# Sixteen meta keys of eight heads turned together, value sums kept per group, and four reordered places in a two-block kernel

## What is computed

```python
def causal_block_attention(q, k, v, scale, cum=None):      # L = 16 meta + 256 real
    def attend(qb, qpos, cq=None):
        s = jnp.einsum('bhqd,bhkd->bhqk', qb, k) * scale
        if cq is not None:
            s = s + (cq[..., :, None] - cum[:, :, None, :])
        s = jnp.where(key_pos[None, :] <= qpos[:, None], s, -jnp.inf)
        p = jax.nn.softmax(s, axis=-1)
        return jnp.einsum('bhqk,bhkd->bhqd', p, v)
...
o_mla = causal_block_attention(q_m, k_m, v_mla, MLA_SCALE)
y_mla = (o_mla * jax.nn.silu(z_mla)) @ w_br_mla[l]
o_fox = causal_block_attention(fq, fk, fv, FOX_SCALE, cum)
y_fox = (o_fox * jax.nn.silu(z_fox)) @ w_br_fox[l]
mixed = (jax.nn.sigmoid(gate_a) * y_mla + jax.nn.sigmoid(gate_b) * y_fox) @ w_out[l]
h = h + rmsnorm_2(mixed, post_norm_g[l])
```

```python
hs = hs * lax.rsqrt(jnp.mean(hs * hs, axis=-1, keepdims=True) + EPS)   # per head
return (hs * norm_w * o_gate) @ w_out
```

## Time and profile before

| | us |
|---|---|
| median of 3 runs | 1001.35 |
| their range | 1000.96 to 1002.16 |
| the profiled execution | 1001.34 |
| its span, first to last instruction | 999.5 |
| PE busy | 957.9 |
| DVE busy | 592.5 |
| ACT busy | 482.3 |
| POOL busy | 22.6 |

### The profile page before, as it was taken

How to read it: one execution, slowest core, us unless ns; L and a number is a source line. 1 busy time by engine, 2 the same in 40 slices (tenths; PEclk the granted TensorE clock), 3 DMA queues, 4 the chain that set the end, 5 groups by cost and what they waited for, 6 DMA issues and landing times.

```text
span 999.5 us, 14170 instructions
## 1 busy us (share of the span) xinstructions
PE 957.9 (96%) x5243; PEld 802.3 (80%) x5243; DVE 592.5 (59%) x1103; ACT 482.3 (48%) x768; POOL 22.6 (2%) x41
## 2 busy tenths in 40 slices
PE   6999799999999999999999999999999999999996
PEld 6877587888888899778888888879988887887875
DVE  4856657745455578556453635776554655665565
ACT  5545546535353447454443434675344444434542
POOL 0003100000000000000000000000000000000000
PEclk9999999999999999999999999999999999999998
DMA  6642245463645522246545464322233233333441
GB/s 215 237 169 85 84 184 180 161 230 148 224 153 198 181 85 86 85 150 224 212 150 228 145 233 173 123 106 107 92 120 127 85 127 127 133 120 127 153 163 43
DMA packets 25319, 149.25 MB, mean 149 GB/s; under 512 B 2992, under 2 KB 3120, under 8 KB 11056
## 3 DMA queue, kind: packets, MB, share of 16 engines
q1 hardware_dynamic: 24624, 146.39, 40.2%
q0 software_dynamic: 640, 2.11, 0.7%
HBM read 147.45 MB, written 1.05 MB: 149 GB/s over the span
## 4 chain that ended last, share of the span: by engine, by line
PE 73%; DVE 7%; ACT 5%; DVEq 3%; issue 2%; ACTq 0%
PE bank L435 21%; PE bank L436 21%; PE bank L437 21%; ACT w_hi L1184 2%; PE bank L506 1%; DVEq L2058 1%; DVE w_lo L1705 1%; PE bank L700 1%; DVE arena L2083 1%; PE bank L983 1%; PE bank L968 1%; PE bank L815 1%; PE bank L1004 1%; PE bank L1005 1%; PE bank L1003 1%
## 5 line engine op out<-in xcount | busy, mean ns | idle before, releaser
L435 PE MATMUL bank<-w_hi,x_hi 128*128 128x512 f32 (+2 forms) x648 | 262.7, 405 | 3.7 <-DVE ffn_nat L1955 1.4
L436 PE MATMUL bank<-w_lo,x_hi 128*128 128x512 f32 (+2 forms) x648 | 254.1, 392 | 0.0
L437 PE MATMUL bank<-w_hi,x_lo 128*128 128x512 f32 (+2 forms) x648 | 252.0, 389 | 0.0
L1619 DVE TENSOR_TENSOR w_lo<-w_raw,w_hi 128x2048 fp32r<-128x2048 f32 x52 | 118.8, 2292 | 62.2 <-ACT w_hi L1123 61.2
L435 PEld LDWEIGHTS bank<-w_hi,x_hi 128*128 128x128 f32 x648 | 122.3, 189 | 33.2 <-issue 5.8
L1705 DVE TENSOR_TENSOR w_lo<-w_raw,w_hi 128x2048 fp32r<-128x2048 f32 x50 | 114.4, 2290 | 51.3 <-ACT w_hi L1184 50.6
L437 PEld LDWEIGHTS bank<-w_hi,x_lo 128*128 128x128 f32 x648 | 121.7, 188 | 27.1
L436 PEld LDWEIGHTS bank<-w_lo,x_hi 128*128 128x128 f32 x648 | 122.0, 188 | 22.4
L1123 ACT ACTIVATE w_hi<-w_raw 128x2048 fp32r<-128x2048 f32 x54 | 103.1, 1916 | 58.4 <-DMA w_raw<-w_main_dram 51.5
L1184 ACT ACTIVATE w_hi<-w_raw 128x2048 fp32r<-128x2048 f32 x50 | 95.0, 1908 | 13.9 <-PE bank L437 9.6
L1323 ACT ACTIVATE ffn_nat<-bank,stat 128x256 f32<-128x256 f32 x44 | 20.8, 473 | 134.2 <-PE bank L437 134.1
(11 more groups left out here) (349 smaller groups left out, 1526.1 us busy)
## 6 DMA issues: line engine op xcount, KB each, us to landing
w_raw<-w_main_dram SPq DMA_DIRECT2D x111, 1024.0 KB, 4.9
s_raw<-w_side_dram SPq DMA_DIRECT2D x51, 512.0 KB, 4.2
h<-x_dram SPq DMA_DIRECT2D x2, 512.0 KB, 3.9
w_raw<-w_main_dram SPq DMA_DIRECT2D x2, 512.0 KB, 6.7
arena<-rows_dram POOLq DMA_DIRECT2D x2, 512.0 KB, 4.1
out_dram<-arena SPq DMA_DIRECT2D x1, 512.0 KB, 2.6
out_dram<-arena SPq DMA_DIRECT2D x2, 256.0 KB, 2.0
arena<-c_b_dram POOLq DMA_DIRECT2D x1, 264.0 KB, 2.8
```

The lines of the kernel that those rows point to most:

```text
L435: pe.matmul(out, ah, bh, start=first, stop=False)
L436: pe.matmul(out, ah, bl, start=False, stop=False)
L437: return pe.matmul(out, al, bh, start=False, stop=last)
L1619: dve.tensor_tensor(w_lo[:, slot, 4 * g:4 * g + 4, :], w_raw[:, g, :, :], w_hi[:, slot, 4 * g:4 * g + 4, :], ALU.subtract).then_inc(w_lo_o ...
```

## The change

It has five parts.

1. First keys: DVE takes the rest of the first half of chunk 1 ahead of the root, and PE turns the root after the first half of the first key matmuls.
2. Recurrent heads: two gate tiles stand ahead of the scores, and the two state matmuls go one behind the other into banks 5 and 7.
3. Output product: the loop is written out. The matmuls of tiles 2 and 3 stand ahead of the turns of tiles 4 and 5; ACT makes tiles 2 and 3 ahead of weights; the gating of heads 2 and 3 signals after each head.
4. Last loop, first heads: the first key block is the first thing in step 0; the side unit of the queries goes ahead of a weight half on DVE; both halves of chunk 39 are split in step 2.
5. Last loop, all heads: `turn` has three transposes and `values` three matmuls. ACT copies the 16 meta columns of each head into a tile of eight heads by 16 keys (`meta_kept`). After eight heads this tile is turned at once (`meta_turn`, two transposes), copied (`meta_turned`) and multiplied by meta values of eight heads set out on a block diagonal (`meta_values`, two matmuls of 512 columns). The diagonal is made by `spread`, a matmul that repeats 16 rows eight times and a DVE product with a mask, once for each 512 columns, in steps 1, 2, 7 and 10. The sums of eight heads stay in banks 6 and 7, and DVE scales them at once (`group_out`).

The core of the diff:

```diff
+GROUP = 8
+SPREADS = {1: ("um", 0), 2: ("um", 1), 7: ("fm", 0), 10: ("fm", 1)}
+def after_rider(n):
+    extra = [SPREADS[n]] if n in SPREADS else []
+    if n and n % GROUP == 0 or n == 2 * NH - 1:
+        extra.append(("mt", n // GROUP if n == 2 * NH - 1 else n // GROUP - 1))
+    return extra
-        keys += RIDERS[n]
+        keys += RIDERS[n][0:1] + after_rider(n) + RIDERS[n][1:]
-        HALVES.setdefault(_at + 1, []).append((_c, 1))
+        HALVES.setdefault(_at + (_c != C_FK + 3), []).append((_c, 1))
+        c_bank = (bank[5], bank[7])
-            pool.memset(f_vm, 0.0).then_inc(vz_ok, 1)
-            pool.memset(v_mm, 0.0).then_inc(vz_ok, 1)
...
+            for k0 in (0, KT // 2):
+                for i in range(2):
+                    for k in range(k0, k0 + KT // 2):
+                        ins = halves_tile(C_MK, None, 2 * i, k, to=bank[6 + i])
+                    if k0:
+                        ins.then_inc(mk_ps, 1)
+                    elif i == 0:
+                        pe.wait_ge(r0_ok, 1)
...
+                gate_part(0, 2)
                 if hh:
                     pe.wait_ge(hf_ok, 2 * hh)
...
-                    pe.matmul(bank[5][:, 0:VW], m_kw[:, d, :], v_aug[:, d, hh, :], ...)
-                    gate_part(beside[d], beside[d + 1])
+                    pe.matmul(c_bank[d][:, 0:VW], m_kw[:, d, :], v_aug[:, d, hh, :], ...)
...
-            streamed("m_out", xn, {4: lambda: pe.wait_ge(xn_ready, 2)}, [m_out_tiles], ahead=False)
+            for k in range(KT):
+                st_wait("m_out", k)
+                if k in (0, 1):
+                    to_stationary("m_out", xn, None, 0, ks=(k + 2,))
+                elif k in (4, 5):
+                    to_stationary("m_out", xn, xn_ready, 3, ks=(k + 2,))
+                m_out_tiles(k)
+                if k == 3:
+                    to_stationary("m_out", xn, xn_ready, 2, ks=(4, 5))
...
-                pe.transpose(bank[5][:, 2 * P:3 * P], s_[:, 2 * M + 2 * P:416], ident[:, :])
-                pe.transpose(bank[6][:, 0:P], s_[:, 0:P], ident[:, :])
-                pe.transpose(bank[6][:, P:2 * P], s_[:, M + P:M + 2 * P], ident[:, :]).then_inc(pt_ps, 1)
+                pe.transpose(bank[5][:, 2 * P:3 * P], s_[:, 2 * M + 2 * P:416], ident[:, :]).then_inc(pt_ps, 1)
+            def values(n, v):
+                pe.wait_ge(pt_ok, A2 + n + 1)
+                first = n % GROUP == 0
+                if first and n:
+                    pe.wait_ge(og_ok, n // GROUP)
+                at = slice(n % GROUP * HD, (n % GROUP + 1) * HD)
+                pe.matmul(bank[6][:, at], pt[:, 0:P], v(0), start=first, stop=False)
+                pe.matmul(bank[7][:, at], pt[:, P:2 * P], v(0), start=first, stop=False)
+                pe.matmul(bank[7][:, at], pt[:, 2 * P:3 * P], v(1), start=False, stop=False)
+            def meta_turn(g):
+                b = acc_wait(("mt", g))
+                pe.wait_ge(mp_ok, GROUP * (g + 1))
+                for r in range(R):
+                    ins = pe.transpose(b[:, r * P:(r + 1) * P], meta_p[g][:, r, :], ident[:, :])
+                done(ins, ("mt", g))
+            def meta_values(g):
+                evacuated(("mt", g), (("um", "fm")[g // 2], g % 2))
+                for r in range(R):
+                    ins = pe.matmul(bank[6 + r][:, :], pt[:, 384 + r * P:384 + (r + 1) * P], meta_v[g], start=False, stop=True)
+                ins.then_inc(og_ps, 1)
+            def spread(key):
+                b = acc_wait(key)
...
+                done(pe.matmul(b[:, :], repeat[0:M, :], src[0:M, key[1] * CH:(key[1] + 1) * CH], start=True, stop=True), key)
...
+                if n == 0:
+                    riders(RIDERS[n], 0)
...
+                last = n % GROUP == 0 and n // GROUP
+                if last:
+                    meta_turn(last - 1)
                 if n:
                     head_values(n - 1)
                 turn(A2 + n)
+                if n in SPREADS:
+                    spread(SPREADS[n])
+                if last:
+                    meta_values(last - 1)
+                if n == 2 * NH - 1:
+                    meta_turn(n // GROUP)
...
             head_values(2 * NH - 1)
+            meta_values(2 * NH // GROUP - 1)
...
+            def meta_kept(n):
+                act.drain()
+                kept = sm[:, n % 2, 0:2 * (M + P)].rearrange("p (r x) -> p r x", r=R)[:, :, 0:M]
+                at = slice(n % GROUP * M, (n % GROUP + 1) * M)
+                act.activation(meta_p[n // GROUP][:, :, at], kept, ACT.Copy).then_inc(mp_ok, 1)
-                meta_turned(A2 + n)
+                meta_kept(n)
+                if n and n % GROUP == 0 or n == 2 * NH - 1:
+                    meta_turned(after_rider(n)[-1][1])
...
             rest_side(0)
+            rest_half(1, 1, 0)
             rstd("x0", [(R, D)])
...
-                ins.then_inc(xn_ready, 1)
+                    if hh:
+                        ins.then_inc(xn_ready, 1)
...
+            rest_side(U_Q)
             rest_half(C_FK + 1, (C_FK + 1) % 2, 1)
-            rest_side(U_Q)
...
+                if n >= 2:
+                    dve.wait_ge(mp_ok, n - 1)
+            def group_out(g):
+                dve.wait_ge(og_ps, g + 1)
+                dve.drain()
...
-                    head_out(n - 1)
+                    head_root(n - 1)
                 dve.wait_ge(pt_ps, A2 + n + 1)
                 dve.tensor_copy(pt[:, 0:384], bank[5][:, 0:384]).then_inc(pt_ok, 1)
+                if n in SPREADS:
+                    spread(SPREADS[n])
+                if n and n % GROUP == 0:
+                    group_out(n // GROUP - 1)
```

More of the change, by code:

```diff
@@ L1268, in _ @@
                     act.wait_ge(c_ps, 2 * hh + d + 1)
-                    act.activation(m_c[:, d, :], bank[5][:, 0:VW], ACT.Copy).then_inc(c_ok, 1)
+                    act.activation(m_c[:, d, :], c_bank[d][:, 0:VW], ACT.Copy).then_inc(c_ok, 1)
                 if hh < H0 - 1:
@@ L1280, in _ @@
             squares(H0 - 1)
[L1281 removed]
+            split_st("m_out", m2_tile, lambda k: pcol("mlstm_norm", k), ks=(2, 3))
+            split_both("m_out", lambda k: pcol("mlstm_norm", k), C_MO + 3, 1, first=4, hi=m2_tile)
             def mixer_out(name, c, ffn_st, gain):
@@ L1807, in gated @@
                 dve.wait_ge(og1_ok, 2 * pair + 2)
-                for r in range(R):
-                    for hh in (2 * pair, 2 * pair + 1):
+                for hh in (2 * pair, 2 * pair + 1):
+                    for r in range(R):
                         xs = XN[:, r, hh * DV:(hh + 1) * DV]
```

111 lines of the change are left out of this document (64 added, 47 removed).

## The result

The changed kernel takes 1014.83 us (median of 4 runs, 1013.98 to 1016.51) against 1001.55 us (4 runs, 1000.96 to 1002.16) of the kernel before: ratio 1.0135, 95% interval 1.0117 to 1.0152. I had forecast 1003.7 and the range ended at 1008.5. The direction was right. The time lies outside the range.

The account below looks back on a forecast made before the run. PE, busy 96% of the span, plus its stands was taken as the bound. Terms summed to +0.2 us on 1001.35, plus 2.2 for one clock fall: 1003.7 us, own range 1000.5 to 1006.5, 8 in 10 from 994.5 to 1008.5.

Parts of the forecast that it names:

- Work of the loop: PE work over 32 heads: 0.67 us less a head, twelve 512-column matmuls and eight transposes added; net -10.2 us.
- Stands of the loop: Last loop: new PE waits at spreads, group ends and riders, plus lost savings, less one removed wait; +16.6 us.
- group end n=8: Last loop: meta value sums wait for ACT's turned meta keys, which stand behind the exps of head 9; 2.25 us.
- second rider of n=3: Last loop: the moved half of chunk 39 puts 2.3 us of DVE ahead of mask and query; +1.25 us.
- Recurrent heads: Recurrent mixer: gate tiles cover the stand at the scores, a second state bank removes another; -1.6 us.
- Output product: Mixer's output: tiles 2 and 3 issued ahead of the 4.77 us wait, gating signalled earlier; -4.9 us.
- First heads: Start of the last loop: query rest ahead of a weight rest, first key block ahead of scores; -0.5 us.
- First keys: Second value chunk: DVE is late, so PE's stand there grows to some 3 us; +0.8 us.
- term of the clock: Stands of 3.85, 2.95 and 3 us in loop and second value chunk: one clock fall, at +2.2 us.
- second rival: Clock falls at all three long stands: 6.6 us instead of 2.2, 1008 us; chance 0.15.
- first rival: Loop: ACT and DVE come sooner, waits at group ends and spreads halve, clock holds; 995.5 us, chance 0.25.
- rival of dear 512-column matmuls: Loop: 512 f32 columns cost twice the price, or value matmuls were covered by weight loads; 1014 us, chance 0.04.

Follow-up runs that it names:

- reorderings alone: Kernel before with the first keys, recurrent heads, output product and first heads changed, without the grouped meta keys: 997.1 us, ratio 0.9952.
- filled stands: Changed kernel with f32 matmuls of a zero weight added on PE inside four loop stands (n=7, 10, 16, 24): 1007.2 us.
- joined kernel with the new first keys: The joined kernel, but with the changed kernel's order of the first keys: 996.6 us.
- gate steps: The joined kernel with the last two gate-tile steps of the last two recurrent heads moved ahead of the fourth value matmul: 993.3 us.
- joined: Changed kernel with ACT's copy ahead of exps, Fox spreads behind riders n=14 and 15, n=8 meta turn and sums later, old first keys: 991.7 us, ratio 0.9896.
- fastest kernel: The joined kernel with spreads behind the riders of n=7, 10, 11 and 14 and over 128 rows: 988.2 us, ratio 0.9866.

## Why the prediction was wrong

Each term of the sum, by the lags of the table:

- Work of the loop: 0.67 us less a head was forecast; the lag falls by 0.66 to 0.69 at the heads from n=11 to n=15 and by 0.60 to 0.69 after n=17, but where a tile rest stands. A pair of sums costs what I had from the earlier trace rows: 0.86 each, 1.88 us for two with the last one's end. A spread costs some 0.3 us more than that: the one of n=2 begins at 693.84 in the changed kernel and the second product behind it at 695.12, 1.28 us later, where 0.86 and a step of 0.12 would be 0.98.
- Stands of the loop. They came about as long as the rows said, together 0.7 us shorter, and one of them elsewhere:

| place | forecast | measured |
|---|---|---|
| spread n=1 | 0.65 | 0.74 |
| spread n=7 | 1.65 | 1.54 |
| group end n=8 | 2.25 | 1.57 |
| spread n=10 | 1.65 | 1.91 |
| group end n=16 | 3.85 | 3.70 |
| group end n=24 | 2.95 | 2.83 |
| three tile rests, each more than before | 0.6 | 0.70, 0.73, 0.71 |
| second rider of n=3 | 1.25 | 0.95 |

The one at n=8 is not the wait that I had described: I expected the value sums to wait for ACT's copy, and PE stood at the turn of the meta keys ahead of them, for the accumulator that DVE frees. The sums did not wait.

- Recurrent heads: -1.6 forecast. The lag falls by 2.2 up to 96.87. But DVE does its root and its weight rest there no sooner, and a stand of 1.59 us at 102.2 took the place of 0.53. In the kernel with the reorderings alone, which has no fall in the way, the heads give -2.9.
- Output product: -4.9 forecast, -4.4 in that kernel, with the stand of 0.96 us that I had at 0.9, and full clock. The -5.8 of the table hold the 1.5 us that come back from the fall at 104.
- First heads: -0.5 forecast, -0.3 measured.
- First keys: +0.8 forecast, with a stand of some 3 us. The stand is 3.18 us; the lag at 56.26 is +1.58, less the 0.36 of the start +1.2. The clock comes on top, 1.6 us.

The loop without its slow stretches: 18.6 less the 9.1 of the filled stands are 9.5, where I had 6.4. The weight rest at 713.68 gave 1.65 where I had 1.5. The 3.1 us that are missing do not lie in the stands. From turn to turn of the probabilities, the five steps with a late spread or a group end (n=7, 8, 10, 16, 24) take 0.5 to 1.0 us more than their stands, their new matmuls and their fall, 3.2 together. Some 0.6 of that are the two spreads in them, by the price above; for the rest my sum has no term, and no run separates what it is. All terms together without the clock miss by +0.4 - 1.3 + 0.5 + 0.2 + 3.1 = +2.9 us.

The step that failed is the term of the clock: "Three lengths lie between; I take one fall, at +2.2." I had two points, a stand of 4.77 us that had a fall behind it and one of 1.50 that had none, and counted as endangered only the three stands near 3 us and above. Measured were six falls, behind 3.18, 1.59, 1.54, 1.91, 3.70 and 2.83 us, that took 1.6, 0.1, 1.6, 3.2, 1.4 and 3.0 us, with the unrounded figures 10.8 in all, 9.1 of it in the loop. With 8.6 too little for the clock, 2.9 for the other terms and 0.4 for the start, 1003.7 becomes 1015.6; the profiled run took 1015.5 and the median is 1014.8. Two errors lie in the 8.6. The three long stands all fell, with 5.9 us instead of 2.2: that is the second rival, which I gave 0.15 and 1008. And 4.9 us came behind three stands of 1.5 to 1.9 us, two of which I had priced by their length and not asked about the clock, although they lay above the one length that I knew to be harmless; the third, at 102, I had not seen, and it cost 0.1. The filled stands show that the 9.1 us of the loop are the clock, not the stands.

The first rival (waits half of mine) fell with the table above. Its argument, that ACT and DVE are half idle, was true and beside the point: ACT stood idle 3.19 us ahead of the exps with the copy behind them in its queue. I had written down that the copy stands behind the exps and took it as given; the remedy was in that sentence. The rival of dear 512-column matmuls named 1014, close to the measured time, by luck: they cost 0.86 us each, not twice that.

## What to carry to other kernels

When a change puts new waits on an engine that was busy 96% of the time, list every stand of about 1.5 us and more that it makes and price each one twice: its own length, and what the clock may take behind it, here 1.4 to 3.2 us where PE had work until the next wait was past, and 0.1 where a wait for ACT of 1.57 us followed and took it up. Before judging an idea by such a version, look at what the releasing engine does ahead of the release: here fewer small matmuls lost 21 us on their own, much of it because a ready copy of 0.36 us stood behind exps in ACT's order (moving it gave 11.7) and because the spreads stood where an accumulator came late. With both moved, and with the same first keys, the grouped keys cost nothing; the spreads behind riders and over 128 rows gave another 3.5 us. Measure a clock effect by filling the stand with work of no use, and read the cost from matched matmuls past the next wait, not from the length of the slow stretch.

## What the runs showed of the hardware

- After the first 12 us, all 16 stands of 2.37 us and more in the traces of this study have a stretch at 1.2 GHz that begins in them or right behind; of those between 1.54 and 1.97 us some were and some not, in code that is the same. The stand of 1.91 us at n=10 has a fall in the changed kernel and none with the copy moved, the one of 1.57 or 1.58 us at n=8 the other way round; the stand of 1.56 to 1.60 us in the recurrent heads has a fall in the changed kernel and none with the reorderings alone. The falls also differ between runs of one kernel: the mean granted clock of ten executions of the kernel with the copy moved lies between 0.988 and 0.993, and their times between 1002.4 and 1006.5 us. Those of the reorderings alone, whose only stands in that range are the ones in the recurrent heads, spread over 0.8. What decides in that range stays open.
- A slow stretch of 3.4 us costs up to half its length, and not always that: 1.6 us at 739 and 1.4 at 824 in the changed kernel, but 0.1 at 104, where the wait for ACT behind it shrank from 1.57 to 0.37 us.
- The clock also fell behind shorter stands where a matmul of 16 rows stood close to them: 0.74 us at 685 in three traces of nine (filled stands, joined kernel with the new first keys, and with the gate steps), and 1.05 us at 804 to 808 in two of three (joined, and with the new first keys). With 128 rows there is one trace with the same two places, and it has neither. Whether the rows decide is not shown.
- In the fastest kernel, with no stand above 1.6 us after the start, the granted clock is full until the tail; with the gate steps moved and the same places of the spreads it still fell once, at 122 us, in a stretch where stands of 0.69, 0.80 and 0.96 us follow each other.
